# Down stage of a two-block transformer kernel: x rows loaded one by one, two weight sums on GpSimd, two step pairs ordered by bank

## What is computed

```python
# first block
gp = dwconv_centered(h @ w_ffn_gate, ffn_conv_w, ffn_conv_b)
x = x + (jax.nn.silu(gp) * (h @ w_ffn_up)) @ w_ffn_down
# second block, then the last norm
ffn = (jax.nn.silu(h2 @ w_ffn_gate) * (h2 @ w_ffn_up)) @ w_ffn_down
x = x + ffn
return rmsnorm(x, norm_f_g)
```

## Time and profile before

| | us |
|---|---|
| median of 3 executions | 3331.39 |
| lowest, highest | 3330.44, 3336.36 |
| the profiled execution | 3336.45 |
| its span, first to last instruction | 3334.7 |
| TensorE busy | 3206.8 (96%) |
| VectorE busy | 2049.6 (61%) |
| ScalarE busy | 1261.9 (38%) |
| GpSimd busy | 904.1 (27%) |
| mean granted TensorE clock | 0.988 |

### The profile page before, as it was taken

The page is one execution under the profiler, slowest core; times in us unless marked ns, Lnnn a source line. Parts: engine busy times, 40 slices in busy tenths (PEclk is TensorE's granted clock), DMA queues, the critical chain, the costliest instruction groups (busy, mean ns, idle before and its releaser), DMA issues.

```text
span 3334.7 us, 61185 instructions
## 1 busy us (share of the span) xinstructions
PE 3206.8 (96%) x26432; PEld 2532.4 (76%) x26432; DVE 2049.6 (61%) x2921; ACT 1261.9 (38%) x2177; POOL 904.1 (27%) x744
## 2 busy tenths in 40 slices
PE   8999999999999998998999999999999999999998
PEld 8678776777777776477788887878777878888777
DVE  5363475666666565847688887662555565655676
ACT  4333334444444432123343343443332333333434
POOL 1231242111111122103567650000000055666200
PEclk9999999999999999999999999999999999999999
DMA  4251244111211211532122247422102412223733
GB/s 150 71 156 45 70 167 150 40 55 48 62 62 44 92 49 56 202 126 82 70 111 108 95 163 244 149 87 95 40 26 96 141 50 105 101 95 114 284 113 114
DMA packets 125004, 344.31 MB, mean 103 GB/s; under 512 B 15600, under 2 KB 16256, under 8 KB 121920
## 3 DMA queue, kind: packets, MB, share of 16 engines
q1 hardware_dynamic: 103584, 255.99, 23.2%
q0 software_dynamic: 21152, 84.42, 6.9%
HBM read 245.46 MB, written 94.90 MB: 102 GB/s over the span
## 4 chain that ended last, share of the span: by engine, by line
PE 81%; DVE 11%; ACT 4%; issue 2%; DMA 1%; POOL 0%; SPq 0%; DVEq 0%; ACTq 0%; POOLq 0%
PE ps L355 42%; PE ps L354 35%; PE ps L358 3%; DVE AR L364 2%; DVE X L364 2%; DVE WS L364 1%; DVE SM L375 1%; DMA AR_b<-h_d 1%; DVE TO L364 1%; DVE HL L364 1%; ACT W L361 1%; ACT HT L1172 1%; DVE HT L368 1%; DVE W L364 1%; ACT AR L361 0%
## 5 line engine op out<-in xcount | busy, mean ns | idle before, releaser
L364 DVE TENSOR_TENSOR WS<-W,WS 128x512 fp32r<-128x512 f32 (+1 forms) x276 | 306.2, 1110 | 278.7 <-ACT WS L361 278.1
L354 PE MATMUL ps<-HH,WS 128*128 128x512 f32 x1280 | 394.6, 390 | 0.0
L354 PE MATMUL ps<-TO,WS 128*128 128x512 f32 x1440 | 349.5, 392 | 6.0 <-DVE WS L364 4.5
L361 ACT ACTIVATE WS<-W 128x512 fp32r<-128x512 f32 (+1 forms) x276 | 204.8, 743 | 321.3 <-PE ps L355 172.8
L354 PEld LDWEIGHTS ps<-TO,WS 128*128 128x128 f32 x1440 | 272.4, 189 | 64.2 <-DVE WS L364 5.3
L354 PEld LDWEIGHTS ps<-HH,WS 128*128 128x128 f32 x1280 | 240.5, 188 | 49.8
L364 POOL TENSOR_TENSOR X<-X 128x512 f32<-128x512 f32 (+1 forms) x80 | 166.7, 2089 | 363.0 <-DVE X L364 275.4
L354 PE MATMUL ps<-HL,WS 128*128 128x512 f32 x640 | 249.6, 390 | 2.8 <-DVE WS L364 2.8
L354 PE MATMUL ps<-TO 128*128 128x512 f32 x936 | 231.9, 396 | 12.9 <-DVE X L364 7.1
L354 PE MATMUL ps<-WS 128*128 128x512 f32 x888 | 217.5, 393 | 3.2 <-DVE WS L364 3.1
L355 PE MATMUL ps<-AR 64*64 64x64 f32 (+2 forms) x5440 | 200.4, 240 | 19.1 <-ACT AR L361 4.7
(11 more groups left out here) (342 smaller groups left out, 6370.7 us busy)
## 6 DMA issues: line engine op xcount, KB each, us to landing
AR_b<-h_d SPq DMA_DIRECT2D x154, 256.0 KB, 2.8
AR<-rw_d SPq DMA_DIRECT2D x104, 256.0 KB, 4.0
W<-in_w_fg SPq DMA_DIRECT2D x44, 512.0 KB, 3.6
W<-in_w_fu SPq DMA_DIRECT2D x44, 512.0 KB, 4.6
h_d<-FST POOLq DMA_DIRECT2D x20, 1024.0 KB, 4.4
x_d<-X POOLq DMA_DIRECT2D x24, 512.0 KB, 4.6
W<-in_w_tok SPq DMA_DIRECT2D x24, 512.0 KB, 3.4
rw_d<-X POOLq DMA_DIRECT2D x40, 256.0 KB, 3.4
```

The lines of the kernel that those rows point to most:

```text
L354: return pe.e.matmul(o, l, r, start=start, stop=stop, skip_group_check=True)
L361: return e.e.activation(o, x, ACT.Copy)
L364: return e.e.tensor_tensor(o, x, y, op)
```

## The change

1. SyncE loads the x tiles one at a time: tiles 0 to 3 in passes 10, 12, 14, 16, tiles 4 to 7 in passes 38, 40, 42, 44, in place of all eight in pass 13. The additions of product 1 move from pass 16 to pass 19.
2. The quarters come in other passes: 21 two passes earlier, 22 one pass earlier, of 12 the tiles 4 to 10 later (pass 17 to 26 in place of 11 to 23).
3. The sums i = 3 and i = 4 leave VectorE. GpSimd makes them, all 11 of i = 3 and then all 11 of i = 4, after its last sums of the hidden tiles. Sum i = 1 of tile k moves on VectorE to other passes (6, 8, 10, 12, 18, 19, 21, 22, 24, 25, 27 for k = 0 to 10, before 5, 7, ... 25).
4. On TensorE the steps 20 and 21 (the last two of product 2) and 64 and 65 (the last two of product 7) are taken bank by bank.

```diff
             hidden(NF - 1)
             last_sums(NF // 2 - 1)
+            for i in (3, 4):
+                for k in range(NF // 2):
+                    weight_sum(ge, f_, i, k)
...
-        ADD_AT = {16: (1, 0), 21: (2, 0), 34: (3, 0), 45: (6, 0), 55: (5, 0), 56: (5, 1), 65: (7, 0), 76: (4, 0)}
+        ADD_AT = {19: (1, 0), 21: (2, 0), 34: (3, 0), 45: (6, 0), 55: (5, 0), 56: (5, 1), 65: (7, 0), 76: (4, 0)}
...
-        QLOADS = sorted([(0 if k < 8 else k - 8, "11", k) for k in range(11)] + [(3 + 2 * k, "12", k) for k in range(11)]
-                        + [(4 + k, "21", k) for k in range(11)] + [(15 + k, "22", k) for k in range(11)])
+        Q12_AT = (3, 5, 7, 9, 17, 18, 20, 21, 23, 24, 26)
+        QLOADS = sorted([(0 if k < 8 else k - 8, "11", k) for k in range(11)] + [(Q12_AT[k], "12", k) for k in range(11)]
+                        + [(2 + k, "21", k) for k in range(11)] + [(14 + k, "22", k) for k in range(11)])
+        XLOADS = {10: 0, 12: 1, 14: 2, 16: 3, 38: 4, 40: 5, 42: 6, 44: 7}
...
-                ae.wait_ge(*at("ve_" + nm, "T", {4: 4, 5: 1, 6: 2, 7: 3}[p], k))
+                ae.wait_ge(*at(("ge_" if p in (4, 7) else "ve_") + nm, "T", {4: 4, 5: 1, 6: 2, 7: 3}[p], k))
...
             elif i == 2:
-                ve.wait_ge(*at("ve_" + nm, "dn", DAT[3, k]))
-                ve.wait_ge(*at("ve_" + nm, "T", 3, k))
+                e.wait_ge(*at("ve_f" + f_, "dn", DAT[3, k]))
+                e.wait_ge(*at("ge_f" + f_, "T", 3, k))
                 o, x, y = q22, q22, q11
...
             for k in range(NF // 2):
-                if n == 5 + 2 * k:
+                if n == Q12_AT[k] + (3 if k < 4 else 1):
                     weight_sum(ve, f_, 1, k)
                 if n == 20 + k:
-                    weight_sum(ve, f_, 3, k)
                     weight_sum(ve, f_, 2, k)
-                if n == 34 + 2 * k:
-                    weight_sum(ve, f_, 4, k)
...
-                if n == 13:
+                if n in XLOADS:
+                    t = XLOADS[n]
                     ffn_half_over(sp, f_)
                     for name in ("dma_st0", "dma_st1", "dma_uv0"):
                         sp.wait_ge(*at(name, f_, NF // 2 - 1))
-                    for t in range(NT):
-                        sp.e.dma_start(xt(t), a["x_d"][t]).then_inc(*dma(f"dma_x{t}", f_))
-                    if f_ == "2":
+                    sp.e.dma_start(xt(t), a["x_d"][t]).then_inc(*dma(f"dma_x{t}", f_))
+                    if f_ == "2" and t == 7:
                         sp.e.dma_start(NFB, row(a["norm_f"])).then_inc(*dma("dma_nf", 0))
...
             last = len(DOWN) - 3
+            by_rows = (DAT[2, NF // 2 - 2], DAT[7, NF // 2 - 2])
             for n in range(last):
                 if n == 67:
                     bk.ready.update(range(4))
+                if n - 1 in by_rows:
+                    continue
                 for j in range(4):
                     product(n, j)
+                    if n in by_rows:
+                        product(n + 1, j)
                     if j % 2:
                         bk.step()
```

More of the change, by code:

```diff
@@ L2485, in down_lo, with weight_sum @@
             tt(ve, o[3], quarter(OF_PRODUCT[p], k), o[2].bitcast(F32), ALU.subtract).then_inc(*ve.sig("ve_" + nm, "dn", n))
-        def weight_sum(ve, f_, i, k):
-            nm = "f" + f_
+        def weight_sum(e, f_, i, k):
             q11, q12, q21, q22 = [quarter(q, k) for q in ("11", "12", "21", "22")]
             if i == 1:
-                ve.wait_ge(*loaded_q(f_, "12", k))
-                ve.wait_ge(*at("ve_" + nm, "dn", DAT[1, k]))
+                e.wait_ge(*loaded_q(f_, "12", k))
+                e.wait_ge(*at("ve_f" + f_, "dn", DAT[1, k]))
                 o, x, y = q11, q12, q11
             elif i == 3:
-                ve.wait_ge(*loaded_q(f_, "22", k))
-                ve.wait_ge(*at("ve_" + nm, "T", 1, k))
+                e.wait_ge(*loaded_q(f_, "22", k))
+                e.wait_ge(*at("ve_f" + f_, "T", 1, k))
                 o, x, y = q12, q22, q12
             elif i == 2:
-                ve.wait_ge(*at("ve_" + nm, "dn", DAT[3, k]))
-                ve.wait_ge(*at("ve_" + nm, "T", 3, k))
+                e.wait_ge(*at("ve_f" + f_, "dn", DAT[3, k]))
+                e.wait_ge(*at("ge_f" + f_, "T", 3, k))
                 o, x, y = q22, q22, q11
             else:
-                ve.wait_ge(*at("ve_" + nm, "dn", DAT[2, k]))
-                ve.wait_ge(*at("ve_" + nm, "T", 2, k))
+                e.wait_ge(*at("ve_f" + f_, "dn", DAT[2, k]))
+                e.wait_ge(*at("ve_f" + f_, "T", 2, k))
                 o, x, y = q21, q21, q22
-            tt(ve, o, x, y, ALU.subtract).then_inc(*ve.sig("ve_" + nm, "T", i, k))
+            tt(e, o, x, y, ALU.subtract).then_inc(*e.sig(e.name + "_f" + f_, "T", i, k))
         def weight_sums(ve, f_, n):
             for k in range(NF // 2):
-                if n == 5 + 2 * k:
+                if n == Q12_AT[k] + (3 if k < 4 else 1):
                     weight_sum(ve, f_, 1, k)
                 if n == 20 + k:
-                    weight_sum(ve, f_, 3, k)
                     weight_sum(ve, f_, 2, k)
-                if n == 34 + 2 * k:
-                    weight_sum(ve, f_, 4, k)
         def down_add(ve, f_, p, which):
@@ L3387, in n1_over @@
             e.wait_ge(*at("ve_f1", "dn", DAT[7, NF // 2 - 1]))
-            e.wait_ge(*at("ve_f1", "T", 4, NF // 2 - 1))
+            e.wait_ge(*at("ge_f1", "T", 4, NF // 2 - 1))
         def tensor_program(pe):
```

## The result

In 15 executions each, the changed kernel has a median of 3345.80 us against 3334.11 of the kernel before, measured in turn: a ratio of 1.0025, with a 95% interval of 1.0015 to 1.0034. A second comparison of the same two (12 executions) gave 1.0018, 1.0007 to 1.0028. The two medians by themselves are 11.7 us apart, which would be 0.35%. So the change makes the kernel slower, by 0.2 to 0.3%. On the scale of the prediction (3331.4 before) the first ratio is 3339.7: inside the range, 4 us above the forecast, and just outside the 0.2% within which I had put it.

What follows compares the result with a forecast made beforehand. TensorE, busy for 96% of the span, was taken to bound the kernel. The terms summed to +1.4 us in f1 and +2.9 in f2, together +4.3 on the median of 3331.4: 3335.7, range 3320 to 3345.

Steps and rivals of the forecast that it cites:

- x loads one by one: Step 18, both down stages: the starvation of the hidden load goes, -3.6 us in f1 and -4.0 in f2.
- The price I named: Pass 10: SyncE waits for GpSimd's last store until about 2012.4; load 15 lands at 2016.3, step 15 hidden by 1 us.
- Sum i = 1 later: Step 9: the split starts in front of GpSimd in f1, -1.0 us; in f2 it may still wait, -0.6.
- The disputed row: Step 9 of f2: VectorE's operation took 3.54 us though begun 0.42 before GpSimd's, against the skill's port rule.
- Bank order: Steps 20/21 and 64/65: late release makes step 66 2.2 us late, +3.4 per stage; step 22 waits 3.4.
- those of product 1 in pass 19 are over by the time of pass 21: Step 22: the additions of product 1, moved to pass 19, were claimed to delay nothing there.
- the lead of three steps covers them: Until pass 27: GpSimd's sums i = 3, one to a pass or rarer, were claimed to be covered.
- GpSimd's sums i = 4: 12 sums back to back make steps 33 and 34 wait 2.0 and 2.4, or 1.4 and 2.4: +4.0 us per stage.
- Rival 1: Passes 27 to 34: GpSimd gets in twice per VectorE operation; +12.3 us, 3343.7; chance 0.27.
- The clock: After TensorE's waits over 2 us a low granted clock costs 1.4 us more a wait in the mean.
- rivals 2, 3 and 4: 2: burst hidden, 3327.7, chance 0.2; 3: bank order costs little, 3316 to 3322, 0.1; 4: DMA wait stays, 3343, 0.08.
- no difference that shows: Whole kernel: 3335.7 us, 0.13% more, within the 0.2% a measurement can tell from no change; chance 0.56.

Runs made afterwards that it cites:

- after: The changed kernel, with the whole change, against the kernel before: ratio 1.0025, median 3345.80 us against 3334.11.
- sums_on_vector: The changed kernel with the sums i = 3 and i = 4 back on VectorE in the old passes, bank order kept: ratio 0.9995 to the kernel before.
- bank_order_only: The kernel before with nothing but the order by bank of steps 20, 21, 64 and 65: ratio 1.0038 to the kernel before, four executions.
- i4_spread: The changed kernel with GpSimd's sums i = 4 each held back to the pass in which VectorE used to make it: ratio 0.9999 to the kernel before.
- the second profile: Profile of the changed kernel run again with no edit: ratio 1.0018 to the kernel before.
- best: Changed kernel's loads, sums on VectorE, old matmul order, additions ahead of the split in passes 21 and 65: ratio 0.9939 to the kernel before.
- loads_only: The changed kernel with the bank order off and the sums i = 3 and i = 4 back on VectorE: ratio 0.9976 to the kernel before.
- adds1_pass17: The changed kernel without bank order, sums on VectorE, and additions of product 1 in pass 17 instead of 19: ratio 0.9966 to the kernel before.
- bank_order_off: The changed kernel with steps 20, 21, 64 and 65 in the old order: ratio 0.9992 to the kernel before.

## Why the prediction was right, and where it wasn't

**x loads one by one: right.** Step 18 waits for nothing. ScalarE's longest wait for a hidden load there is now 4.54 us in place of 10.98. The price I named is in SyncE's timeline of f1:

```profile
2013.10 0.33 SPq L2566 DMA_DIRECT2D AR_b<-h_d  x1
2013.47 0.74 SPq L2556 DMA_DIRECT2D AR_b<-in_w_fd  x1
2018.98 0.33 SPq L2583 DMA_DIRECT2D X<-x_d  x1
```

It stands for 4.8 us in pass 10 until 2018.98, in this profile, which is 7.5 us later in all, so 2011.5 where I had 2012.4. The load of step 15 is there at 2022.98 (2015.5; I had 2016.3). VectorE ends its split at 2024.93, and the step is due at 2026.86 and, since step 10 was late, starts at 2027.50: hidden, by 2 us and not by 1.

**Sum i = 1 later: right in direction, not in size.** In f1 step 9 is on time, but step 10 now waits 0.31 and loses 0.64, since the sum stands ahead of its split; I had not looked one step further, and -0.4 is left of the -1.0. In f2 the wait is 1.81 in place of 2.42, as I took it, but no low clock followed as before, so that the gain is 2.3 and not 0.6. The disputed row came again: VectorE's split at 3134.22, the operation now in that place, took 3.53 though GpSimd's sum began 0.42 after it.

```profile
3134.22 3.53 DVE L364 TENSOR_TENSOR WS<-AR_b,WS 128x512 fp32r<-128x512 f32 x1
...
3134.64 1.31 POOL L364 TENSOR_TENSOR FST<-X 128x512 f32<-128x512 f32 x1
...
3135.90 2.97 POOL L364 TENSOR_TENSOR FST<-X,FST 128x512 f32<-128x512 f32 x2
```

Its 3.53 are 2.85 more than the 0.68 that it takes alone, about what two of GpSimd's operations take (1.3 and 1.5).

The rule of the Trainium skill ("SBUF — State Buffer", SBUF: two separate sides) that whichever operation starts first keeps the shared port doesn't describe this start as the profile dates it; its other half, that the loser waits for the whole of the other's instruction, is what the turns at steps 31 to 34 show.

**Bank order: the price at step 66 to a tenth, at step 22 the wrong share.** Step 66 waits 2.06 + 0.16 = 2.2, as worked out, in every kernel with the order by bank and the additions behind the split (after, sums_on_vector, bank_order_only, i4_spread), and nothing with the order off or with the additions first. At step 22 the wait of 3.4 came as 3.60 and 3.26. But the step "those of product 1 in pass 19 are over by the time of pass 21" failed. They are over, but VectorE is still behind from them: without the bank order step 22 waits 3.31 with three sums, and 1.95 once these additions stand in pass 17. So the additions in pass 19 cost 1.36 there. The order by bank adds 0.9 in f2 (3.26 against 2.35) and 0.7 with the sums on VectorE (3.99 against 3.31), not 2.0. The cost of pass 19 was hidden in my sum behind the larger one: the total was right and the reason half wrong.

In f1 of the changed kernel the late release isn't even what binds at step 22. VectorE's rows, the split of step 24 in f1, in f2, and an earlier one of f1:

```profile
2032.46 3.48 DVE L364 TENSOR_TENSOR WS<-AR_b,WS 128x512 fp32r<-128x512 f32 x2
...
2047.07 0.68 DVE L364 TENSOR_TENSOR TO<-AR_b,TO 128x512 fp32r<-128x512 f32 x1
...
3175.15 0.69 DVE L364 TENSOR_TENSOR TO<-AR_b,TO 128x512 fp32r<-128x512 f32 x1 [0.78 <-ACT TO L361]
```

In f2 it waits for ScalarE, as I had it. In f1 it would have been let in at 2041.10 + 4.76 + 0.87 = 2046.73 and comes at 2047.07 without a wait: it has had no pause since 2028.95, and in that time five of its operations took 1.1 us more beside GpSimd's sums i = 3. So "the lead of three steps covers them" failed as well, by the 0.3 to 0.7 us that f1 (3.60, 3.98 in the second profile) waits longer than f2 (3.26 in both). That part was not tested by itself.

**GpSimd's sums i = 4: right.** Turns at 1.7, 12 operations back to back, the wait at steps 33 and 34. The sizes: 0.36 and 2.02 in f1 against 1.4 to 2.0 and 2.4, then 0.33 at step 35. With the clock it was 3.7 in f1 and 4.6 in f2 for the 4.0 I took (4.7 in both in the second profile). i4_spread and sums_on_vector both take the waits away. Rival 1 (GpSimd gets in twice for each operation of VectorE's) did not happen in the burst: after GpSimd's first sum of 1.61 every operation of both engines there takes 1.72 to 1.78.

**The clock** is the term with the largest error. I gave each wait over 2 us 1.4 us more. In f1 step 22 took 5.46 and step 23 3.24, 2.9 us more than 2.88 each; the window from 2050 to 2055 has a granted clock of 0.50, which is 1.2 of 2.4 GHz:

```profile
2050.00:2055.00 5.00, 4.70 (x11) 3.77 (x12) 4.35 (x8) 0.00 (x0) 1.48 (x2) 0.50 0.64 216
```

Step 66 took 1.7 more in f1 and 0.1 in f2, after the same wait of 2.06. The mean over the six waits over 2 us after is 1.4, as I took it, but a single profile can differ by several us in this alone.

**The sum and the claim.** What each term came to in the first profile, in us, clock losses included:

| term | f1 forecast | f1 measured | f2 forecast | f2 measured |
|---|---|---|---|---|
| sum i = 1 later (steps 9, 10) | -1.0 | -0.36 | -0.6 | -2.26 |
| x loads (step 18) | -3.6 | -3.60 | -4.0 | -3.99 |
| step 22 | -1.4 | +0.50 | +0.1 | +0.42 |
| burst (steps 33 to 35) | +4.0 | +3.67 | +4.0 | +4.65 |
| step 66 | +3.4 | +3.64 | +3.4 | +2.05 |
| stage | +1.4 | +3.85 | +2.9 | +0.87 |

Together that is +4.7 for +4.3, and the second profile gives +3.4. That the total is so near is luck in part: f1 is 2.5 above and f2 2.0 below, mostly by the clock. The two timings give +8.3 and +6.0 us with intervals from +2.3 to +11.3. So the mechanisms, but for step 22, and the sign of the sum were right, and rivals 2, 3 and 4 are refuted by steps 33, 66 and 15. The forecast "no difference that shows" was too cautious: it shows, barely. What lies between 4.7 and the timed 8 is not located. But every one of the thirteen comparisons has its time above what the stage losses say, by 0.5 us (best) to 7 (bank_order_only), with loads_only, adds1_pass17 and i4_spread at 4 to 6. All of them share one profile of the kernel before, so this points to a profile of that kernel with some us more loss than usual; one profile of it can't show that, and the clock outside the stages is the other candidate. It stays open. Nor were the new passes of the weight quarters tried apart from the x loads.

## What to carry to other kernels

Ask of a reordering what it signals later, not only what it finishes earlier: the order by bank completes a bank sooner and frees the slot of the step before 2 us later, and here the engine that should profit stood behind just that slot. Where an engine with spare time is late, look first at the order of its own work: the additions that everybody waited for cost nothing to move ahead of a split due three steps later, and brought 0.2% alone and 0.3% on top of the new loads. Work given to GpSimd while VectorE reads two operands from SBUF was free when placed in VectorE's gaps, one operation at a time, and cost 3.7 to 4.7 us a stage in one burst.

## What the runs showed of the hardware that I had not expected

- GpSimd's sum costs VectorE nothing when it starts at the end of a split and fits into the gap: 1.29 us in a gap of 1.43, with VectorE's splits around it at 0.68 to 0.69; of the 22 sums i = 4 in i4_spread only two met an operation of VectorE that reads SBUF alone, which then took 1.37.
- Turns are not the only way the two engines meet. In i4_spread, f1, a GpSimd sum dated 2045.33 took 2.82 us in place of 1.3 while VectorE's next two operations, at 2045.72 and 2046.32, stayed at 0.68; at step 9 of f2 it was VectorE that stood behind two of GpSimd's.
- After equal waits of 2.06 us TensorE's next step took 4.58, 3.00 and 3.01 us in different stages and kernels: what a wait costs beyond its length is 0.1 or 1.7 us in most cases, and 2.6 to 2.9 in three (3.60 after, 3.20 in bank_order_off, 3.99 in sums_on_vector), where a window of 5 us has a granted clock of 0.50 to 0.54. The length doesn't decide: after 3.99 in f2 of sums_on_vector it was 1.7.
- The first 1980 us, the same code in every kernel, differ by 11 us between single profiles (1975.3 to 1986.1), more than the effect under study; only differences within a stage could be compared from one profile each.
